# Moving columns read from the two halves of the operand in turn, on one Trainium2 core

## The chip, the core and the metric

The kernel runs on one core of a Trainium2 chip. The time is device microseconds (us) of one execution. A core has TensorE (PE; its weight loads are listed apart, as PEld), VectorE (DVE), ScalarE (ACT), GpSimd (POOL) and SyncE (SP, here the queue that issues the loads). A TensorE product holds 128 columns of one operand in the array (the stationary one, put there by a weight load) and streams the other through it column by column (the moving one); each moving column gives one column of sums in PSUM, at the place that the output pattern gives it. All operands lie in SBUF, 128 partitions by some number of 4-byte elements.

## The reference, cut to what matters

Two attention layers and a third block with a gated feed-forward net, on 256 tokens of width 2048. Nearly all arithmetic is in the products of activations with weights:

```python
# first block, twice (l = 0, 1)
h = x @ w_in                                  # (256, 2048) @ (2048, 6672)
# y_a, y_b, y_m: band attention, gated linear attention, memory attention
...
mkv = mem @ w_mem_kv                          # (256, 2048) @ (2048, 1024)
y = jnp.concatenate([y_a * jax.nn.silu(a_z), y_b * jax.nn.silu(b_z), y_m * jax.nn.silu(m_z)], axis=-1)
x = layer_norm(DEEPNORM_ALPHA * x + y @ w_out, ln_g, ln_b)
# second block
h = rms_norm(x, norm_mix_pre)
proj = h @ w_in_2                             # (256, 2048) @ (2048, 11272)
# y_a: hgrn2 recurrence, y_b: forgetting attention
...
merged = jax.nn.sigmoid(g_a) * (y_a @ w_up_a) + jax.nn.sigmoid(g_b) * (y_b @ w_up_b)
x = x + rms_norm(merged @ w_o, norm_mix_post)
gate, up = jnp.split(rms_norm(x, norm_ffn_pre) @ w_ffn_in, 2, axis=-1)      # width 2 * 5632
x = x + rms_norm((jax.nn.silu(gate) * up) @ w_ffn_down, norm_ffn_post)
```

## The kernel before

All inputs are float32. Each operand of a large product is split into a high part (rounded to the type fp32r, which TensorE takes in one pass) and the low rest, `hi + lo`, and a product is three: hi times hi, lo times hi, hi times lo. The activations lie in a `Split` tensor (`xx`, `yy`, `mem`), in which each tile of 128 features has 256 columns of high part (one a token) and then 256 of low part. Weights come by a load of 512 KB into one of five `raw` buffers; ACT makes the high part (`make_hi`, L441, `wh`) and DVE the low one (`make_lo`, L613, `wl`), each into one of four buffers.

There are two forms of large product. In **form f** (`unit_f`) the weights are stationary and the activations move, and a row of the sums is an output feature: `hi_row` moves `act.both(k)`, the 512 columns of high and low part, and `lo_row` moves `act.hi_of(k)`, 256 columns, onto the second half of the bank. The true sum is then the first half of the bank plus the second. In **form t** (`unit_t`, `last_rows`) the activations are stationary and 512 columns of `wh` or `wl` move, and a row of the sums is a token. `narrow` is form f for 16 or 8 output columns. All go through `add` (L283), so that L283 in the profile is every large product. A product is one matmul instruction of 128x512 or 128x256. Small products (attention scores, L368; transposes, L379; values, L387; the levels of the linear attention, `level`, L407) take plain float32 and go other ways; in the profile each of their instructions has two records.

The sums of form f are read by `join`: ACT copies the second halves of two banks into the destination (L460) and DVE adds the first halves (L638, or L640 where a factor is wanted). Those of form t are read by `evacuate` (L465 ACT, L648 DVE), `scale_value` (L574 ACT), `add_layer` (L780 DVE), `weigh_post` (L865 DVE) and `first_product` (L884 DVE); those of `narrow` by `narrow_sum`. Column c of a bank is column c of what moved. Products fill the bank pairs 0-1 and 2-3 by turns, so that a pair is read while the other is filled.

One place in the kernel of before already moves columns that do not lie side by side. `level(a, s, ...)` moves, in the third block, the second half of every group of `2*s` columns, for s = 64, 32, 16, 8, 4, 2, 1 and then (no s) all columns: 64 columns in runs of s. `merge_level` (L750) then reads PSUM in the same runs with a COPY_PREDICATED on DVE, and `differences` (L724, L725) reads and writes SBUF in such runs.

The order of the instructions on each engine is the order in which the program text issues them. Nothing is planned from costs.

Of the kernel before, what the change touches and what calls it, by code (L numbers as in the profile page):

```python
# [6 lines left out]
D, S, P = 2048, 256, 128  # L7
# [4 lines left out]
ALPHA = float(np.float32(4.0 ** 0.25))  # L12
# [49 lines left out]
class Split:  # L62
# [14 lines left out]
        return self.part(k, n, 1)  # L77

    def both(self, k):
        k += self.first  # L80
        return self.tensor[:, 2 * S * k:2 * S * (k + 1)]

    def hi_of(self, k, c=0, n=S):
        k += self.first
# [5 lines left out]

def tiled(x):
    return x.rearrange("p (k s) -> p k s", s=S)

def halves(x, s):
# [65 lines left out]
def build(nc, A, out):  # L161
    f32, f32r, i32 = mybir.dt.float32, mybir.dt.float32r, mybir.dt.int32
    ALU, ACT, AX = mybir.AluOpType, mybir.ActivationFunctionType, mybir.AxisListType
    ctx = ExitStack()
    with ctx:
# [59 lines left out]
        pairs = [ctx.enter_context(nc.psum_tensor(f"banks{n}", [P, 1024], f32)) for n in range(4)]  # L225
        banks = [pairs[n // 2][:, 512 * (n % 2):512 * (n % 2) + 512] for n in range(8)]
# [33 lines left out]
        def over2(row):  # L260
            return row.rearrange("p (o s) -> p o s", o=1).to_broadcast([P, 2, S])
# [6 lines left out]

        def of_bank_pair(pr):

            return pairs[pr[0] // 2][:, :].rearrange("p (t o s) -> p t o s", t=2, o=2)

        class Tensor(Part):

# [10 lines left out]
            def unit_f(self, h, l, act, pr, u, nu, made_hi, made_lo, free, hi_read, lo_read):  # L285

                def hi_row(*waits):
                    self.wait_ge(made_hi, *waits)
                    for kk in range(4):  # L290
                        k = 4 * u + kk
                        for t in range(2):
                            c = kk * S + t * P
                            i = self.add(banks[pr[t]], h[:, c:c + P], act.both(k), k == 0, k == 4 * nu - 1 and u % 2 == 1)
                    i.then_inc(hi_read.sem, 1)

                def lo_row(*waits):
                    self.wait_ge(made_lo, *waits)
                    for kk in range(4):
                        k = 4 * u + kk  # L300
                        for t in range(2):
                            c = kk * S + t * P
                            i = self.add(banks[pr[t]][:, S:2 * S], l[:, c:c + P], act.hi_of(k), False,
                                         k == 4 * nu - 1 and u % 2 == 0)
                    i.then_inc(lo_read.sem, 1)

                if u % 2 == 0:
                    hi_row(*free)
                    lo_row()
                else:  # L310
                    lo_row(*free)
                    hi_row()

            def unit_t(self, h, l, tiles, made_hi, made_lo, free, hi_read, lo_read):

                self.wait_ge(made_hi, *free)
                for b, act, t, k, place, start, _ in tiles:
                    m = h[:, place * 512:place * 512 + 512]
                    self.add(banks[b], act.hi_of(k, t * P, P), m, start, False)
                    i = self.add(banks[b], act.lo_of(k, t * P, P), m, False, False)  # L320
                i.then_inc(hi_read.sem, 1)
                self.wait_ge(made_lo)
                for b, act, t, k, place, _, stop in tiles:
                    i = self.add(banks[b], act.hi_of(k, t * P, P), l[:, place * 512:place * 512 + 512], False, stop)
                i.then_inc(lo_read.sem, 1)

            def last_rows(self, tiles, free, done):

                self.wait_ge(*free)
                for b, act, t, k, place, h, l, stop in tiles:  # L330
                    c = slice(place * 512, place * 512 + 512)
                    self.add(banks[b], act.hi_of(k, t * P, P), h[:, c], False, False)
                    self.add(banks[b], act.lo_of(k, t * P, P), h[:, c], False, False)
                    i = self.add(banks[b], act.hi_of(k, t * P, P), l[:, c], False, stop)
                i.then_inc(done.sem, 1)

            def narrow(self, bank, weights, act, free, done):
# [92 lines left out]
        class Scalar(Part):  # L430
# [26 lines left out]

            def join(self, pr, dst, scale, row, summed, free, copied, sums):
                self.wait_ge(summed, *free)
                self.e.activation(tiled(dst), of_bank_pair(pr)[:, :, 1, :], ACT.Copy,  # L460
                                  scale=1.0 if scale is None else scale).then_inc(copied.sem, 1)

            def evacuate(self, pr, dst, summed, first, second):
                self.wait_ge(summed)
                self.e.activation(dst[:, 0:512], banks[pr[0]], ACT.Copy).then_inc(first.sem, 1)  # L465

            def narrow_sum(self, b, n, dst, tmp, bias, row, summed, free, copied, sums):
                self.wait_ge(summed, *free)
                self.e.activation(dst, banks[b][0:n, S:2 * S], ACT.Copy).then_inc(copied[0].sem, 1)
                self.e.activation(tmp, banks[b][32:32 + n, 0:S], ACT.Copy).then_inc(copied[1].sem, 1)  # L470

            def exp_of_minus_abs(self, z, tmp, made, free, steps):
                self.wait_ge(*made, *free)
# [97 lines left out]

            def scale_value(self, o, b, factor, summed, free, done):
                self.wait_ge(summed, factor[1], *free)
                self.e.activation(o, banks[b], ACT.Identity, scale=factor[0]).then_inc(done.sem, 1)  # L574

            def forget_exps(self, u, tmp, made, first, second):
                self.wait_ge(made)
# [27 lines left out]
        class Vector(Part):  # L605
# [26 lines left out]
                self.e.tensor_scalar(lb[4], lb[3], -1.0, 1.0, ALU.mult, ALU.add).then_inc(made[6].sem, 1)  # L632

            def join(self, pr, dst, scale, row, summed, free, copied, sums):
                d, first = tiled(dst), of_bank_pair(pr)[:, :, 0, :]
                self.wait_ge(copied)
                if scale is None:
                    self.e.tensor_tensor(d, first, d, ALU.add).then_inc(sums[0].sem, 1)  # L638
                else:
                    self.e.scalar_tensor_tensor(out=d, in0=first, scalar=scale, in1=d, op0=ALU.mult,  # L640
                                                op1=ALU.add).then_inc(sums[0].sem, 1)
                if row is not None:
                    self.wait_ge(sums[0], row[1])
                    self.e.tensor_tensor(d, d, over2(row[0]), ALU.mult).then_inc(sums[1].sem, 1)

            def evacuate(self, pr, dst, summed, first, second):
                self.wait_ge(summed)
                self.e.tensor_copy(dst[:, 512:1024], banks[pr[1]]).then_inc(second.sem, 1)  # L648

            def narrow_sum(self, b, n, dst, tmp, bias, row, summed, free, copied, sums):  # L650
                self.wait_ge(copied[0])
                self.e.tensor_tensor(dst, banks[b][0:n, 0:S], dst, ALU.add).then_inc(sums[0].sem, 1)
                self.wait_ge(copied[1], sums[0])
                self.e.tensor_tensor(dst, dst, tmp, ALU.add).then_inc(sums[1].sem, 1)
                if bias is not None:
                    self.wait_ge(sums[1], row[1])
                    self.e.tensor_tensor(dst, dst, row[0][0:n, :], ALU.mult).then_inc(sums[2].sem, 1)
                    self.wait_ge(sums[2])
                    self.e.tensor_scalar(dst, dst, bias, None, ALU.add).then_inc(sums[3].sem, 1)
# [117 lines left out]

            def add_layer(self, z, bank, stats, summed, loaded, added, taken):
                self.wait_ge(summed, *loaded)
                self.e.scalar_tensor_tensor(out=z, in0=z, scalar=ALPHA, in1=banks[bank], op0=ALU.mult, op1=ALU.add).then_inc(added.sem, 1)  # L780
                self.wait_ge(added)
                self.e.bn_stats(stats, z).then_inc(taken.sem, 1)

# [78 lines left out]

            def weigh_post(self, o, b, w, made, done):
                self.wait_ge(*made)
                self.e.tensor_tensor(o, banks[b], w, ALU.mult).then_inc(done.sem, 1)  # L865

            def sum_squares(self, total, parts, made, done):
                self.wait_ge(*made)
# [6 lines left out]
            def gate_half(self, u, z, row, sigmoid, made, done):  # L875
                self.wait_ge(sigmoid)
                self.e.tensor_tensor(u, z, u, ALU.mult).then_inc(made.sem, 1)
                if row is not None:
                    self.wait_ge(made, row[1])
                    self.e.tensor_tensor(tiled(u), tiled(u), over2(row[0]), ALU.mult).then_inc(done.sem, 1)  # L880

            def first_product(self, o, b, factor, u, made, done):
                self.wait_ge(*made)
                self.e.scalar_tensor_tensor(out=o, in0=banks[b], scalar=factor[0], in1=u, op0=ALU.mult, op1=ALU.mult).then_inc(done.sem, 1)  # L884

        class Gpsimd(Part):

# [1621 lines left out]
```

## Time and profile before

| | us |
|---|---|
| median of 3 runs | 2407.21 (2406.29 to 2407.24) |
| profiled execution | 2406.68 |
| its span, first to last instruction | 2404.9 |
| PE busy in it | 2392.9 |
| DVE busy | 1541.9 |
| ACT busy | 1283.0 |

The profile page gives busy time of each engine, the span in 40 slices, and groups of instructions by line. A record of a matmul covers more than the time for which it holds the engine, since one begins before the last one's end: how long a product takes of TensorE's time is seen in a stretch of many, from start to start.

### The profile page before, as it was taken

To read this page: it belongs to the slowest core of one execution; us is meant where nothing else is said; L and a number is where in the kernel's file an instruction comes from. 1 tells how busy PE (TensorE), PEld (TensorE's weight loads), DVE (VectorE), ACT (ScalarE), POOL (GpSimd) and SP (SyncE) were. 2 spreads that over 40 slices of the span, in tenths; PEclk is the share of its full clock that TensorE was granted. 3 is DMA by queue.
4 is the path that set the end of the run, shared out by engine and by line. 5 is a ranking of instruction groups with operands and counts; after the bars stand their busy time and mean duration, and the time that the engine had idled before them with its cause. 6 is when DMAs were issued, how large, how long until landed. Compare 5 with 4: busy or idle time off the path is not lost.

```text
span 2404.9 us, 32960 instructions
## 1 busy us (share of the span) xinstructions
PE 2392.9 (99%) x13053; PEld 2067.0 (86%) x13053; DVE 1541.9 (64%) x1753; ACT 1283.0 (53%) x1741; POOL 12.3 (1%) x17
## 2 busy tenths in 40 slices
PE   9999999999999999999999999999999999999998
PEld 7888888888888888888888888888888888888887
DVE  6566567665665777686675567766666666665555
ACT  5444566444445654656654457555655555554444
POOL 0000000000000000000000000000000000000000
PEclk9999999999999999999999999999999999999999
DMA  8545447665445574554454545585555556557554
GB/s 305 198 151 165 166 164 266 214 223 186 157 142 178 189 285 144 197 187 153 167 175 152 174 157 184 188 284 186 183 193 193 184 184 202 183 194 251 195 192 141
DMA packets 130058, 458.84 MB, mean 191 GB/s; under 512 B 13776, under 2 KB 20464, under 8 KB 127984
## 3 DMA queue, kind: packets, MB, share of 16 engines
q1 hardware_dynamic: 128944, 450.39, 55.3%
q0 software_dynamic: 816, 6.29, 0.7%
q8 instruction: 102, 1.67, 0.3%
q14 instruction: 52, 0.43, 0.1%
q10 hardware_dynamic: 144, 0.07, 0.0%
HBM read 448.30 MB, written 8.39 MB: 190 GB/s over the span
## 4 chain that ended last, share of the span: by engine, by line
PE 97%; DVE 2%; ACT 1%; issue 0%; DMA 0%; SPq 0%; DVEq 0%; ACTq 0%
PE banks L283 91%; PE banks L407 2%; PE banks L387 1%; PE banks L368 1%; DVE wl L613 1%; PE banks L347 1%; PE banks L379 0%; ACT wh L441 0%; DMA raw<-in_kv_t 0%; DVE yy L617 0%; PE banks L418 0%; PE banks L419 0%; PE banks L417 0%; PE banks L395 0%; DVE b L775 0%
## 5 line engine op out<-in xcount | busy, mean ns | idle before, releaser
L613 DVE TENSOR_TENSOR wl<-raw,wh 128x1024 fp32r<-128x1024 f32 x776 | 938.2, 1221 | 410.5 <-ACT wh L441 405.0
L441 ACT ACTIVATE wh<-raw 128x1024 fp32r<-128x1024 f32 (+1 forms) x779 | 803.2, 1051 | 358.8 <-PE banks L283 209.6
L283 PE MATMUL banks<-xx,wh 128*128 128x512 f32 (+1 forms) x3760 | 906.6, 392 | 0.0
L283 PEld LDWEIGHTS banks<-xx,wh 128*128 128x128 f32 (+1 forms) x3760 | 686.0, 187 | 137.6 <-issue 0.7
L283 PEld LDWEIGHTS banks<-xx,wl 128*128 128x128 f32 x3712 | 479.9, 191 | 20.7 <-DVE wl L613 1.2
L283 PE MATMUL banks<-xx,wl 128*128 128x256 f32 x3712 | 495.0, 284 | 0.6 <-DVE wl L613 0.5
L283 PE MATMUL banks<-wh,xx 128*128 128x512 f32 x1504 | 376.5, 390 | 0.0
L283 PEld LDWEIGHTS banks<-wh,xx 128*128 128x128 f32 x1504 | 280.9, 188 | 57.6
L283 PE MATMUL banks<-wl,xx 128*128 128x512 f32 x752 | 204.0, 389 | 0.0
L283 PEld LDWEIGHTS banks<-wl,xx 128*128 128x128 f32 x752 | 141.2, 188 | 29.4
L283 PE MATMUL banks<-wh,yy 128*128 128x512 f32 x416 | 103.2, 389 | 0.0
L283 PEld LDWEIGHTS banks<-wh,yy 128*128 128x128 f32 x416 | 78.0, 188 | 16.2
L283 PE MATMUL banks<-yy,wh 128*128 128x512 f32 x256 | 61.2, 391 | 0.0
L283 PE MATMUL banks<-wl,yy 128*128 128x512 f32 x208 | 55.9, 389 | 0.0
L283 PEld LDWEIGHTS banks<-yy,wh 128*128 128x128 f32 x256 | 47.0, 188 | 9.1
L460 ACT ACTIVATE z<-banks 128x512 f32<-128x512 f32 x24 | 14.3, 598 | 74.4 <-PE banks L283 71.8
L460 ACT ACTIVATE hraw<-banks 128x512 f32<-128x512 f32 x20 | 12.0, 598 | 77.1 <-PE banks L283 77.1
L613 DVE TENSOR_TENSOR xl<-raw,xh 128x1024 fp32r<-128x1024 f32 x32 | 38.6, 1222 | 21.2 <-ACT xh L441 20.8
L441 ACT ACTIVATE xh<-raw 128x1024 fp32r<-128x1024 f32 x32 | 33.3, 1059 | 31.0 <-PE banks L283 17.2
L638 DVE TENSOR_TENSOR hraw<-banks,hraw 128x512 f32<-128x512 f32 x20 | 13.9, 693 | 54.6 <-ACT hraw L460 54.6
L283 PEld LDWEIGHTS banks<-wl,yy 128*128 128x128 f32 x208 | 39.1, 188 | 8.1
L638 DVE TENSOR_TENSOR z<-banks,z 128x512 f32<-128x512 f32 x24 | 16.6, 692 | 44.8 <-ACT z L460 44.8
(280 smaller groups left out, 1882.1 us busy)
## 6 DMA issues: line engine op xcount, KB each, us to landing
raw<-in_w_in_f SPq DMA_DIRECT2D x304, 512.0 KB, 3.4
raw<-in_w_ffn_f SPq DMA_DIRECT2D x160, 512.0 KB, 3.9
raw<-in_w_ffn_down SPq DMA_DIRECT2D x88, 512.0 KB, 4.3
raw<-in_w_in_t SPq DMA_DIRECT2D x80, 512.0 KB, 3.4
raw<-in_w_out_t SPq DMA_DIRECT2D x64, 512.0 KB, 4.8
raw<-in_w_o_t SPq DMA_DIRECT2D x32, 512.0 KB, 4.5
raw<-in_kv_t SPq DMA_DIRECT2D x16, 512.0 KB, 5.3
raw<-in_kv_f SPq DMA_DIRECT2D x16, 512.0 KB, 5.3
```

The source lines that it names most:

```text
L283: return self.e.matmul(bank, stationary, moving, start=start, stop=stop, skip_group_check=True)
L347: i = self.e.transpose(banks[bank][:, j * P:(j + 1) * P], tile, ident)
L368: i = self.e.matmul(o, a.q(h)[:, t * P:t * P + P], a.k(h)[:, 0:nk], start=True, stop=a.decay is None)
L387: i = self.e.matmul(banks[4][:, h * P:(h + 1) * P], a.v(kt, h), pt, start=(kt == 0), stop=(kt == nt - 1))
L407: j = self.e.matmul(part(banks[6 + i][:, n * P:(n + 1) * P]), lk[r, c:c + P], part(rq[r, c:c + P]), start=True, stop=True)
L441: self.e.activation(hi, source, ACT.Copy).then_inc(done.sem, 1)
L460: self.e.activation(tiled(dst), of_bank_pair(pr)[:, :, 1, :], ACT.Copy, scale=1.0 if scale is None else scale).then_inc(copied.sem, 1)
L613: self.e.tensor_tensor(lo, source, hi.bitcast(f32), ALU.subtract).then_inc(done.sem, 1)
L638: self.e.tensor_tensor(d, first, d, ALU.add).then_inc(sums[0].sem, 1)
```

## The change

Every large product takes its moving columns in another order. `in_turn` views n columns as two halves and takes column 0 of the first half, column 0 of the second, column 1 of the first, and so on. `act.both(k)` becomes the high part in turn and then the low part in turn (halves of 128 columns, so each column lies 512 bytes from the one before); `act.hi_of(k)` becomes `act.hi_in_turn(k)` in `lo_row`; in form t the 512 columns of weights are read in turn (halves of 256 columns, 1,024 bytes apart). The count of columns, the stationary operands, the PSUM addresses written and the sums are the same, but column 2b + a of a bank now holds what was column b of half a. So every reader of such a bank views it with `in_order`, reading each second element, and views what it writes `by_half`; in SBUF all stays where it was. `join` with a factor needs a pattern of more dimensions than the instruction has, and is written as two instructions of half the size (six places, L640). The order of instructions on all engines is otherwise the same.

```diff
     def both(self, k):
         k += self.first
-        return self.tensor[:, 2 * S * k:2 * S * (k + 1)]
+        return self.tensor[:, 2 * S * k:2 * S * (k + 1)].rearrange("p (o a b) -> p o b a", o=2, a=2)
+
+    def hi_in_turn(self, k):
+        return in_turn(self.hi_of(k))
...
+def in_turn(x):
+    return x.rearrange("p (a b) -> p b a", a=2)
+
+def in_order(x):
+    return x.rearrange("p (b a) -> p a b", a=2)
+
+def by_half(x):
+    return x.rearrange("p (a b) -> p a b", a=2)
+
+def tiled_by_half(x):
+    return x.rearrange("p (k a b) -> p k a b", a=2, b=P)
...
         def of_bank_pair(pr):
-            return pairs[pr[0] // 2][:, :].rearrange("p (t o s) -> p t o s", t=2, o=2)
+            return pairs[pr[0] // 2][:, :].rearrange("p (t o b a) -> p t o a b", t=2, o=2, a=2)
...
@@ unit_f @@
-                            i = self.add(banks[pr[t]][:, S:2 * S], l[:, c:c + P], act.hi_of(k), False,
+                            i = self.add(banks[pr[t]][:, S:2 * S], l[:, c:c + P], act.hi_in_turn(k), False,
...
@@ unit_t @@
-                    m = h[:, place * 512:place * 512 + 512]
+                    m = in_turn(h[:, place * 512:place * 512 + 512])
...
-                    i = self.add(banks[b], act.hi_of(k, t * P, P), l[:, place * 512:place * 512 + 512], False, stop)
+                    i = self.add(banks[b], act.hi_of(k, t * P, P), in_turn(l[:, place * 512:place * 512 + 512]), False, stop)
...
@@ join, ACT @@
-                self.e.activation(tiled(dst), of_bank_pair(pr)[:, :, 1, :], ACT.Copy,
+                self.e.activation(tiled_by_half(dst), of_bank_pair(pr)[:, :, 1, :, :], ACT.Copy,
...
@@ join, DVE @@
-                d, first = tiled(dst), of_bank_pair(pr)[:, :, 0, :]
+                d, first = tiled_by_half(dst), of_bank_pair(pr)[:, :, 0, :, :]
...
-                    self.e.scalar_tensor_tensor(out=d, in0=first, scalar=scale, in1=d, op0=ALU.mult,
-                                                op1=ALU.add).then_inc(sums[0].sem, 1)
+                    for k in range(2):
+                        i = self.e.scalar_tensor_tensor(out=d[:, k], in0=first[:, k], scalar=scale, in1=d[:, k], op0=ALU.mult,
+                                                        op1=ALU.add)
+                    i.then_inc(sums[0].sem, 1)
...
@@ add_layer; evacuate, scale_value, weigh_post, first_product and narrow_sum are changed alike @@
-                self.e.scalar_tensor_tensor(out=z, in0=z, scalar=ALPHA, in1=banks[bank], op0=ALU.mult, op1=ALU.add).then_inc(added.sem, 1)
+                self.e.scalar_tensor_tensor(out=by_half(z), in0=by_half(z), scalar=ALPHA, in1=in_order(banks[bank]), op0=ALU.mult,
+                                            op1=ALU.add).then_inc(added.sem, 1)
```

## Rows read from the trace of the kernel before

**Rows 1.** The page, busy time and share of the span by engine.

```profile
PE 2392.9 (99%) x13053; PEld 2067.0 (86%) x13053; DVE 1541.9 (64%) x1753; ACT 1283.0 (53%) x1741; POOL 12.3 (1%) x17
```

**Rows 2.** Busy time by stretch, L283 alone: start:end, length, busy (records), clock, DMA.

```profile
0.00:2405.00 2405.00, 2271.91 (x11792) 1932.09 (x11792) 1.00 0.56 191
```

**Rows 3.** Groups of instructions, shapes apart: the large products of 256 columns.

```profile
L283 PE MATMUL banks<-xx,wl 128*128 128x256 f32 x3712 | 495.0, 284 | 0.6 <-DVE wl L613 0.5
...
L283 PE MATMUL banks<-yy,wl 128*128 128x256 f32 x256 | 33.2, 283 | 0.0
...
L283 PE MATMUL banks<-mem,wl 128*128 128x256 f32 x128 | 17.6, 285 | 0.3
```

**Rows 4.** Timeline of PE: start us, length us, what, count.

```profile
258.27 2.08 PE L283 MATMUL banks<-xx,wl 128*128 128x256 f32 x16
...
2201.34 1.98 PE L283 MATMUL banks<-wh,xx 128*128 128x512 f32 x8
2203.15 1.07 PE L283 MATMUL banks<-wl,xx 128*128 128x512 f32 x4
```

**Rows 5.** One line's records, L283: duration ns min/median/max, first and last start.

```profile
L283 PE MATMUL banks<-xx,wl x3712: 277/283/468, 57.9 to 2155.9; 128*128 128x256 f32 x196
...
L283 PE MATMUL banks<-wl,xx x752: 388/389/400, 81.4 to 2396.9; 128*128 128x512 f32 x188
```

**Rows 6.** Small products on the timeline of PE: levels s = 64, 2, 1, and all columns.

```profile
1034.47 1.89 PE L407 MATMUL banks<-lqe 128*128 128x64 f32 x16
...
1112.56 1.90 PE L407 MATMUL banks<-lqe 128*128 128x64 f32 x16
1128.27 1.89 PE L407 MATMUL banks<-lqe 128*128 128x64 f32 x16
1135.66 1.95 PE L407 MATMUL banks<-q,k 128*128 128x128 f32 x16
```

**Rows 7.** One line's records: scores of 256 columns, and the first products of the program.

```profile
L368 PE MATMUL banks<-mk,q x8: 377/379/381, 628.1 to 629.6; 128*128 128x256 f32 x8
...
L279 PE MATMUL banks<-asleep x11: 390/628/792, 1.1 to 5.5; 128*128 128x512 f32 x11
```

**Rows 8.** Timeline of DVE, runs of 8, 4, 2 and 1 elements (L750), 4 and 1 (L724).

```profile
1083.10 0.76 DVE L750 COPY_PREDICATED lacc<-cst,banks 128x256 f32<-128x256 int32 x2 [2.98 <-PE banks L407]
1089.31 0.69 DVE L724 TENSOR_TENSOR le<-b 128x512 f32<-128x512 f32 x1
...
1100.16 0.76 DVE L750 COPY_PREDICATED lacc<-cst,banks 128x256 f32<-128x256 int32 x2
...
1115.49 1.33 DVE L750 COPY_PREDICATED lacc<-cst,banks 128x256 f32<-128x256 int32 x2
1118.37 0.70 DVE L724 TENSOR_TENSOR le<-b 128x512 f32<-128x512 f32 x1
...
1130.49 1.31 DVE L750 COPY_PREDICATED lacc<-cst,banks 128x256 f32<-128x256 int32 x2
```

**Rows 9.** Busy time by stretch: `join`'s copy L460 (ACT), its sum L638 (DVE).

```profile
0.00:2405.00 2405.00, 81.17 (x136) 1.00 0.56 191
...
0.00:2405.00 2405.00, 89.71 (x130) 1.00 0.56 191
```

**Rows 10.** What PE waited for: us in total, times, longest us.

```profile
PE banks L283 <- ACT wh L441: 1.2, 2, 0.9
...
PE banks L283 <- DVE wl L613: 0.5, 1, 0.5
```

**Rows 11.** Chain of work that ended last, in order of time: start us, us, what.

```profile
2394.85 2.51 PE banks L283 x11
...
2397.38 0.70 ACT junk L557 x2
...
2398.17 0.69 DVE o_buf L865
```

More of the change, by code:

```diff
@@ L331, in last_rows @@
                     c = slice(place * 512, place * 512 + 512)
-                    self.add(banks[b], act.hi_of(k, t * P, P), h[:, c], False, False)
-                    self.add(banks[b], act.lo_of(k, t * P, P), h[:, c], False, False)
-                    i = self.add(banks[b], act.hi_of(k, t * P, P), l[:, c], False, stop)
+                    self.add(banks[b], act.hi_of(k, t * P, P), in_turn(h[:, c]), False, False)
+                    self.add(banks[b], act.lo_of(k, t * P, P), in_turn(h[:, c]), False, False)
+                    i = self.add(banks[b], act.hi_of(k, t * P, P), in_turn(l[:, c]), False, stop)
                 i.then_inc(done.sem, 1)
@@ L464, in evacuate @@
                 self.wait_ge(summed)
-                self.e.activation(dst[:, 0:512], banks[pr[0]], ACT.Copy).then_inc(first.sem, 1)
+                self.e.activation(by_half(dst[:, 0:512]), in_order(banks[pr[0]]), ACT.Copy).then_inc(first.sem, 1)
             def narrow_sum(self, b, n, dst, tmp, bias, row, summed, free, copied, sums):
                 self.wait_ge(summed, *free)
-                self.e.activation(dst, banks[b][0:n, S:2 * S], ACT.Copy).then_inc(copied[0].sem, 1)
-                self.e.activation(tmp, banks[b][32:32 + n, 0:S], ACT.Copy).then_inc(copied[1].sem, 1)
+                self.e.activation(by_half(dst), in_order(banks[b][0:n, S:2 * S]), ACT.Copy).then_inc(copied[0].sem, 1)
+                self.e.activation(by_half(tmp), in_order(banks[b][32:32 + n, 0:S]), ACT.Copy).then_inc(copied[1].sem, 1)
             def exp_of_minus_abs(self, z, tmp, made, free, steps):
@@ L573, in scale_value @@
                 self.wait_ge(summed, factor[1], *free)
-                self.e.activation(o, banks[b], ACT.Identity, scale=factor[0]).then_inc(done.sem, 1)
+                self.e.activation(by_half(o), in_order(banks[b]), ACT.Identity, scale=factor[0]).then_inc(done.sem, 1)
             def forget_exps(self, u, tmp, made, first, second):
@@ L639, in join @@
                 else:
-                    self.e.scalar_tensor_tensor(out=d, in0=first, scalar=scale, in1=d, op0=ALU.mult,
-                                                op1=ALU.add).then_inc(sums[0].sem, 1)
+                    for k in range(2):
+                        i = self.e.scalar_tensor_tensor(out=d[:, k], in0=first[:, k], scalar=scale, in1=d[:, k], op0=ALU.mult,
+                                                        op1=ALU.add)
+                    i.then_inc(sums[0].sem, 1)
                 if row is not None:
                     self.wait_ge(sums[0], row[1])
+                    d = tiled(dst)
                     self.e.tensor_tensor(d, d, over2(row[0]), ALU.mult).then_inc(sums[1].sem, 1)
@@ L647, in evacuate @@
                 self.wait_ge(summed)
-                self.e.tensor_copy(dst[:, 512:1024], banks[pr[1]]).then_inc(second.sem, 1)
+                self.e.tensor_copy(by_half(dst[:, 512:1024]), in_order(banks[pr[1]])).then_inc(second.sem, 1)
             def narrow_sum(self, b, n, dst, tmp, bias, row, summed, free, copied, sums):
                 self.wait_ge(copied[0])
-                self.e.tensor_tensor(dst, banks[b][0:n, 0:S], dst, ALU.add).then_inc(sums[0].sem, 1)
+                self.e.tensor_tensor(by_half(dst), in_order(banks[b][0:n, 0:S]), by_half(dst), ALU.add).then_inc(sums[0].sem, 1)
                 self.wait_ge(copied[1], sums[0])
@@ L864, in weigh_post @@
                 self.wait_ge(*made)
-                self.e.tensor_tensor(o, banks[b], w, ALU.mult).then_inc(done.sem, 1)
+                self.e.tensor_tensor(by_half(o), in_order(banks[b]), by_half(w), ALU.mult).then_inc(done.sem, 1)
             def sum_squares(self, total, parts, made, done):
@@ L883, in first_product @@
                 self.wait_ge(*made)
-                self.e.scalar_tensor_tensor(out=o, in0=banks[b], scalar=factor[0], in1=u, op0=ALU.mult, op1=ALU.mult).then_inc(done.sem, 1)
+                self.e.scalar_tensor_tensor(out=by_half(o), in0=in_order(banks[b]), scalar=factor[0], in1=by_half(u), op0=ALU.mult,
+                                            op1=ALU.mult).then_inc(done.sem, 1)
         class Gpsimd(Part):
```

## The prediction

> **What bounds the kernel now.** I read the busy times first: PE is busy for 2392.9 us of a span of 2404.9, DVE for 64% of it and ACT for 53% [rows 1]. Then the waits: PE waits for ACT's and DVE's splitting of weights for 1.2 and 0.5 us in all [rows 10]. So the time is TensorE's own work, and nearly all of it is line 283, the large products, with 2271.9 us [rows 2]. What one costs is read from start to start. Sixteen products of 256 columns take 2.08 us, the last one's record being 0.283 us, so one takes (2.08 - 0.283) / 15 = 0.120 us. Eight of 512 columns take 1.98 us with a record of 0.389, so one takes (1.98 - 0.389) / 7 = 0.227 us [rows 4, 5]. The difference, 0.107 us for 256 columns, is 0.418 ns a column: the 2.4 GHz at which the clock stands in the whole run (1.00 in [rows 2]) is 0.417 ns a column. What is left, 0.120 - 0.107 = 0.013 us, is the same for both sizes: a fixed part of each product. In the count, 3,712 + 256 + 128 = 4,096 products have 256 columns [rows 3] and the other 11,792 - 4,096 = 7,696 have 512 [rows 2], which makes 4,096 x 256 + 7,696 x 512 = 4,989,000 moving columns. They come to 4.989 M x 0.417 ns = 2,079 us, and the fixed parts to 11,792 x 0.0133 = 157 us, 2,236 of the 2,272. **A column already goes at the array's own rate.** A new order of columns can't make it faster; it can only leave it, or slow it.
>
> **The moving reads.** All 4.989 M columns are now read from alternate places, 512 or 1,024 bytes apart. No row of before shows such a read. The bounds: from below, it costs nothing, since TensorE still asks for one element a column from each partition. From above, by the nearest rows: the levels of the linear attention move 64 columns in runs of s, and at s = 1 every second element. Their 16 records take 1.89 us at s = 64 and 1.89 at s = 1, and 1.95 with 128 columns side by side [rows 6]. That would look like "runs don't matter", but it isn't: since 64 and 128 columns take the same, something else sets the pace there, the weight load. What the row gives is a cap. A record takes (1.89 - 0.275) / 15 = 0.108 us, up to 0.112 by the row of 128 columns. A record of 256 columns in plain float32 takes (629.6 - 628.1) / 7 = 0.214 us [rows 7], twice the 0.107 of 256 columns in one pass, so a record is two passes, and the record at s = 1 reads 128 columns, in at most 0.112 us: 0.875 ns each. Elements that don't lie side by side could thus cost up to 2.1 times as much as now with nothing in this trace to show for it. The value between: 0.417 ns is the shortest time at which anything here takes an element (DVE takes 512 in 0.69 us, 1.35 ns each [rows 8]), and whatever the read path gives in pairs or lines of neighbours is needed most there. The natural loss is that a fetch which served two columns serves one, hence two cycles for a column, 0.833 ns. The other row at about that price is the first products of the program, 0.44 us from start to start for 512 columns, 0.86 ns each [rows 7]. I take 0.833: 4.989 M x (0.833 - 0.417) = **+2,079 us**. The cap gives 4.989 M x (0.875 - 0.417) = +2,285 us. The fixed 157 us stay.
>
> A sentence of the skill speaks for a loss. The Trainium skill, "Advanced Engine Details and Errata", section Memory Cachelines, says that SBUF has lines of 16 bytes, that at least two accesses should hit one line to hide the memory's latency, and that a different line for each access is penalised; "in turn" makes each access another line than the one before. It gives no price. At s = 1 above, steps of 8 bytes leave two hits in a line, so the trace neither agrees nor disagrees. Another speaks against it, and is the first rival.
>
> **The readers.** A bank is read at every second element. DVE's COPY_PREDICATED reads PSUM so in the levels: two of 256 elements take 0.76 us in runs of 8 and of 4, and 1.33 and 1.31 in runs of 2 and 1 [rows 8], so 0.57 us more for 512 elements. The other row, a TENSOR_TENSOR within SBUF, takes 0.69 us in runs of 4 and 0.70 in runs of 1 [rows 8]: nothing. So a read of 512 elements costs 0 to 0.57 us more. There are 130 + 6 sums of `join` (L638, L640), 8 copies, 16 + 16 + 2 others on DVE, 178, and on ACT 136 + 8 + 10 = 154 (L638 and L460 in [rows 9], the others by the order of the instructions): 0 to 101 us on DVE and 0 to 88 us on ACT. I take the middle, but it hardly counts. The cover is that a bank pair is filled while the other is read: form f fills a pair with 32 products of 512 columns and 32 of 256, 32 x 0.347 = 11.1 us, and one `join` is 0.60 + 0.69 = 1.3 us (81.17 / 136 and 89.71 / 130 [rows 9]), 2.4 at most. DVE would go from 64% to 68%. On the path are the last read of the kernel (L865, 0.69 us [rows 11]) and some ten places where a norm follows a product: 0 to 11 x 0.57 = 6 us, taken as 1. The six split instructions add six fixed parts on DVE, below 1 us together, and are covered too. If TensorE becomes twice as slow, everything on DVE, ACT and the loads has twice the time, and PE's present 12 us of idleness (2404.9 - 2392.9) may shrink: -6 us.
>
> **Sum.** Against the profiled execution's 2406.7 us, 0.5 below the median: 2406.7 + 2,079 + 1 - 6 = **4,481 us**, with 4,460 to 4,700 as its own range (the cap gives 4,687).
>
> **The rivals.** (1) *The hop is free*; it ends on the other side. TensorE's read stream keeps both places open, or its buffer fetches ahead, and a column stays at 0.417 ns. What remains is the readers: 2407.2 + 0 to 6, about 2,408 us. It decides if a read of 128 partitions by one element is no slower than by two neighbours. For it: L724 shows no loss in runs of 1 on DVE [rows 8], and only two streams alternate. Against it: L750 does lose [rows 8], and TensorE reads 3.2 times as fast as DVE. Beside it stands a rule: the Trainium skill, "Vector Engine (DVE) Microarchitecture Reference", section 5.2, tells that a one-source operation whose read stream alternated between two regions 16 KiB apart at every element went at the full read rate, though hops in other patterns cost some two thirds more. If TensorE's port behaves like that, this rival holds; no row here shows it. (2) *The fixed part goes.* If the 0.013 us of each product come from where its moving columns are read (a clash with the weight load that runs beside it), another order could save up to 157 us: 2,250 us. Against it: they are the same for 256 and 512 columns, and for activations and weights as the moving side (1.07 us for four of 512: (1.07 - 0.389) / 3 = 0.227 again [rows 4]), so they look like a change of weights, not like a clash of addresses. (3) *A hop costs TensorE what short runs cost L750*, 0.57 us / 512 = 1.1 ns an element: + 4.989 M x 1.1 = 5,550 us, about 7,960 us. For it: it is the only row in which short runs cost anything. Against it: the cap at s = 1 rules it out for steps of 8 bytes, though not for 512. (4) A loss of a part only, such as the first columns of each product: 2,450 to 4,400 us.
>
> **How the numbers follow.** Half rate 0.46; free 0.27; the fixed part shrinks 0.12; far worse than half rate 0.10; a part 0.05. The forecast is the likeliest, 4,481 us. The range has to leave out no more than 2 in 10: from 2,250 (rival 2's end, with rivals 1 and 4 in it) to 4,700, which leaves out rival 3 and what a wider miss of the price would be. It is wide because two answers lie 2,000 us apart with little between. A measurement of this kernel can tell about 0.2%, 5 us, from no change. Faster by more: 0.12 of rival 2 and 0.01 of rival 1; within: 0.20 of rival 1; slower: the rest of rival 1 (0.06, the readers on the path) and 0.61 of the others.
>
> **What would show it.** Half rate: eight products of 512 columns in a row take (1.98 - 0.39) x 440 / 227, some 3.1 us from first to last start instead of 1.6, sixteen of 256 columns 15 x 0.227 = 3.4 instead of 1.8; the weight loads' share falls from 86% to about 46%, DVE's to about 35%. Free: the same rows unchanged. The readers: L460 and L638 at 597 and 690 ns or up to 0.57 us more. The fixed part: 256 columns below 0.120 us by as much as 512 below 0.227. The prediction is wrong at its root if the price of a column doesn't follow from neighbours in SBUF, and in size if the fetch is wider than two elements.

## The result

The changed kernel takes 2289.84 us (2288.61 to 2291.24, four runs) where the kernel before takes 2407.22 (2406.29 to 2407.89): 0.9513 of it, with a 95% interval of 0.9496 to 0.9529. It is 117 us faster; the forecast was 2,074 us slower. The nearest of the prediction's times is that of rival 2, a smaller part beside the columns in each product.

The page of the profile after, busy time by engine (answers to [rows 1]), and the stretch of the whole run for the large products alone, which are line 305 now (answers to [rows 2]):

```profile
PE 2272.6 (99%) x13053; PEld 2044.5 (89%) x13053; DVE 1543.5 (67%) x1759; ACT 1278.3 (56%) x1741; POOL 12.3 (1%) x17
```

```profile
0.00:2290.00 2290.00, 2151.59 (x11792) 1910.91 (x11792) 1.00 0.61 200
```

The same number of products at the same granted clock (1.00) takes 2151.6 us instead of 2271.9. The timeline of PE of the kernel after (answers to [rows 4]) and two lines of its records (answers to [rows 5]) show where:

```profile
246.78 1.95 PE L305 MATMUL banks<-xx,wl 128*128 128x256 f32 x16
248.56 1.89 PE L305 MATMUL banks<-xx,wh 128*128 128x512 f32 x8
...
252.01 1.03 PE L305 MATMUL banks<-wl,xx 128*128 128x512 f32 x4
```

```profile
L305 PE MATMUL banks<-xx,wh x3760: 379/379/634, 51.0 to 2053.4; 128*128 128x512 f32 x195, 128*48 128x512 f32 x3
...
L305 PE MATMUL banks<-xx,wl x3712: 271/275/460, 56.1 to 2051.7; 128*128 128x256 f32 x196
```

A product of 512 columns takes (1.89 - 0.379) / 7 = 0.216 us from start to start, where it took 0.227; one of 256 columns takes (1.95 - 0.275) / 15 = 0.112, where it took 0.120. The sum closes: 7,696 x 0.011 + 4,096 x 0.008 = 85 + 33 = 118 us, and the times differ by 117. In the profiled executions the large products' busy time falls by 2271.9 - 2151.6 = 120.3 us, and PE's idle time grows from 2404.9 - 2392.9 = 12.0 us to 2289.2 - 2272.6 = 16.6.

The readers of the sums, which now take each second element of PSUM, cost nothing (the answers to [rows 9], in the form of one line's records; ACT's copy and DVE's sum in `join`):

```profile
L482 ACT ACTIVATE z<-banks x24: 592/597/601, 1340.0 to 2032.8; 128x512 f32<-128x512 f32 x24
```

```profile
L660 DVE TENSOR_TENSOR z<-banks,z x24: 682/692/692, 1340.6 to 2033.5; 128x512 f32<-128x512 f32 x24
```

They were at 597 and 690 ns on average before. PE still waits for ACT and DVE for a few microseconds only (2.0 and 2.8 us for the weights; 1.2 and 0.5 in [rows 10]).

### The profile page after: what moved, and what is told of

It is laid out like the page before. It is cut to its first block, busy times and chain, and to the rows that moved or that the text cites. A ratio compares the mean times of both kernels' runs of the same rounds, so it can differ in the third digit from the quotient of the medians.

```text
span 2289.2 us, 32966 instructions
## 1 busy us (share of the span) xinstructions
PE 2272.6 (99%) x13053; PEld 2044.5 (89%) x13053; DVE 1543.5 (67%) x1759; ACT 1278.3 (56%) x1741; POOL 12.3 (1%) x17
## 4 chain that ended last, share of the span: by engine, by line
PE 95%; DVE 2%; DMA 2%; ACT 1%; issue 0%; SPq 0%; DVEq 0%; ACTq 0%
PE banks L305 89%; PE banks L429 2%; PE banks L409 1%; PE banks L390 1%; DVE wl L635 1%; PE banks L369 1%; PE banks L401 0%; ACT wh L463 0%; DMA raw<-in_kv_f 0%; DMA w_bc<-in_norm_mix_post 0%; DMA raw<-in_memT 0%; DVE yy L639 0%; DMA raw<-in_xT 0%; DMA raw<-in_kv_t 0%; PE banks L441 0%
## 5 line engine op out<-in xcount | busy, mean ns | idle before, releaser
L305 PE MATMUL banks<-xx,wh 128*128 128x512 f32 (+1 forms) x3760 | 860.8, 380 | 0.0
L305 PEld LDWEIGHTS banks<-xx,wl 128*128 128x128 f32 x3712 | 456.2, 192 | 17.6 <-DVE wl L635 3.5
L305 PE MATMUL banks<-xx,wl 128*128 128x256 f32 x3712 | 466.5, 276 | 2.3 <-DVE wl L635 2.2
L305 PE MATMUL banks<-wh,xx 128*128 128x512 f32 x1504 | 359.9, 380 | 0.0
L305 PE MATMUL banks<-wl,xx 128*128 128x512 f32 x752 | 195.9, 379 | 0.0
L660 DVE TENSOR_TENSOR z<-banks,z 128x512 f32<-128x512 f32 x24 | 16.6, 691 | 37.9 <-ACT z L482 37.9
```

The lines of the kernel that those rows point to most:

```text
L305: return self.e.matmul(bank, stationary, moving, start=start, stop=stop, skip_group_check=True)
```

## The experiments

Two questions: which property of the moving order makes a product 11 ns quicker, and why the halves in turn, whose every element lies 512 or 1,024 bytes from the last, don't cost double. Three kernels that leave the computation out and run trains of products on an otherwise idle core ask this; four others are the whole kernel with a part of the change or another order.

### Trains of products, one order each

The edit is a kernel of its own. Each line issues 32 products, each with its own stationary tile and moving tile out of eight and seven, and each line has its own number in the profile:

```python
for i in range(N): e.matmul(B(i), W(i), M(i), **k)                 # plain 512
for i in range(N): e.matmul(B(i), W(i), turn(M(i)), **k)           # two halves in turn
for i in range(N): e.matmul(B(i), W(i), runs(M(i), 2), **k)        # halves in turn, by pairs of neighbours
...
```

> This kernel leaves the whole computation out: it runs trains of 32 products (64 in the first), each train on a line of its own, on an otherwise idle chip, and copies x to the output. Start to start per product is read. Known from the two kernels: plain 512 columns 227 ns, in turn 216; plain 256 120, in turn 112. Theory A, a clash of the moving read with the weight load that runs beside it: another order of the stationary read (every fourth column) moves the 227 as well, the same operands each time give less than 227, and 48 stationary columns give less than 128 do. Theory B, neighbours in the moving stream are what costs (each product pays for its first fetch of neighbours): pairs, runs of 4 and of 8 from two halves in turn stay at 227 or lie between, in turn and even-then-odd are at 216. Theory C, it is the pattern's number of dimensions and not the addresses: two far runs of 256 already give 216, and step 2 in one dimension stays at 227. Theory D, it is the other engines' traffic in the whole kernel: here plain and in turn are equal. In bfloat16 A and D expect a difference too; B and C say nothing.

The timeline of PE: start us, length us, line, count. From the start of one line to that of the next, divided by 32, is the time of a product. Lines 66 to 70 are the halves in turn by 1, 2, 4, 8 and 16 neighbours; 72 two far runs of 256; 73 each second column; 74 all even columns, then all odd; 75 the four quarters in turn; 88 the order 0, 4, 1, 5, 2, 6, 3, 7 within each group of 8; 89 plain, one element on. All are fp32r.

```profile
34.56 7.07 PE L66 MATMUL banks<-xr,wr 128*128 128x512 f32 x32
41.46 11.04 PE L67 MATMUL banks<-xr,wr 128*128 128x512 f32 x32
52.33 8.18 PE L68 MATMUL banks<-xr,wr 128*128 128x512 f32 x32
60.35 7.95 PE L69 MATMUL banks<-xr,wr 128*128 128x512 f32 x32
68.13 7.84 PE L70 MATMUL banks<-xr,wr 128*128 128x512 f32 x32
...
83.09 7.42 PE L72 MATMUL banks<-xr,wr 128*128 128x512 f32 x32
90.34 14.66 PE L73 MATMUL banks<-xr,wr 128*128 128x512 f32 x32
104.83 14.69 PE L74 MATMUL banks<-xr,wr 128*128 128x512 f32 x32
...
215.69 7.07 PE L88 MATMUL banks<-xr,wr 128*128 128x512 f32 x32
222.60 7.70 PE L89 MATMUL banks<-xr,wr 128*128 128x512 f32 x32
```

| moving order, fp32r, 512 columns | ns a product |
|---|---|
| plain | 227 to 228 |
| two halves in turn | 216 |
| halves in turn, by pairs / by 4 / by 8 / by 16 / by 64 | 340 / 251 / 243 / 240 / 228 |
| two far runs of 256 | 227 |
| each second column; all even, then all odd | 453; 453 |
| quarters in turn; 64 parts in turn | 274; 431 |
| 0, 4, 1, 5, 2, 6, 3, 7 within each 8 | 216 |
| plain, the same operands each time; same stationary; same moving | 227; 227; 227 |

Theory D (traffic of the other engines) falls: alone on the core the two orders differ by the same 11 ns. Theory C (the number of dimensions) falls by line 72, which has two dimensions and 227 ns. Theory A, the clash with the weight load, is weakened: the same operands each time take 227 ns like any others, and 48 stationary columns take 236 ns plain, more and not less. (Its other part told nothing: with a stationary tile read at steps a product takes 233 to 238 ns, and 234 even with 256 moving columns, so something else than the moving read sets the pace there.) Theory B expected pairs between 216 and 227, and they take 340, and even-then-odd at 216, which takes 453: it falls as it was put. So neighbours in the stream don't hurt as such, and a hop doesn't either; what they have to do with each other was open.

### Two streams

Column by column, halves in turn looks like the worst order for a memory that gives neighbours together. Looked at as two streams, the columns with even numbers and those with odd ones, it is the best: each walks through neighbours. Plain gives each stream every second element. This kernel tells the two views apart; its trains read, among others:

```python
# halves in turn, step 2 in each: even columns 0, 2, 4, ...; odd columns 512, 514, ...
xr[:, c:c + 1024].rearrange("p (a b c) -> p b a c", a=2, c=2)[:, :, :, 0]
# in turn within each 4: 0, 2, 1, 3
M(i).rearrange("p (g a b) -> p g b a", a=2, b=2)
```

> Like m1_patterns this kernel leaves the whole computation out and runs trains of 32 products. Seen there: plain 227 ns for 512 columns, in turn 216, pairs of neighbours from the two halves 340, runs of 4 250, step 2 453. Theory S (two streams): TensorE fetches the even columns and the odd columns of the moving operand as two streams, each of which is quick if its own elements are neighbours and slow if each lies in another piece of memory. It expects: halves in turn with step 2 in each like plain (227), with step 4 in each like step 2 (some 450), in turn within 4 elements (0, 2, 1, 3: each stream goes in pairs) like plain or worse, within 16, 32 and 128 like the halves (216), eighths in turn slower than 272. Theory O (one stream, where alternation as such is free): halves in turn with step 2 like step 2 alone (453). For the fixed 11 ns: if they are a clash with the weight load, they shrink with fewer stationary columns (16 columns: below 218) and don't grow with the moving columns (264 plain 11 over 264 in turn); if they are the stream's own, they grow with the moving columns (384: 8, 264: 6). Start one to sixteen elements on: by a clash of addresses between moving and stationary reads, something between 216 and 240 that depends on the start; in turn 216 at each start.

The timeline of PE again; 75, 76, 77 and 79 are plain with 480, 448, 384 and 264 columns, 80 and 82 in turn with 384 and 264, 83 plain, one element on; 90 is in turn within each 4 columns, 91 within each 16, 92 within each 32, 95 eighths in turn, 96 halves in turn with step 2 in each, 97 the same with step 4, 98 step 4 alone:

```profile
92.48 7.10 PE L75 MATMUL banks<-xr,wr 128*128 128x480 f32 x32
99.42 6.65 PE L76 MATMUL banks<-xr,wr 128*128 128x448 f32 x32
105.91 5.73 PE L77 MATMUL banks<-xr,wr 128*128 128x384 f32 x32
...
116.17 4.05 PE L79 MATMUL banks<-xr,wr 128*128 128x264 f32 x32
120.05 5.36 PE L80 MATMUL banks<-xr,wr 128*128 128x384 f32 x32
...
129.60 3.76 PE L82 MATMUL banks<-xr,wr 128*128 128x264 f32 x32
133.20 7.71 PE L83 MATMUL banks<-xr,wr 128*128 128x512 f32 x32
...
184.26 7.46 PE L90 MATMUL banks<-xr,wr 128*128 128x512 f32 x32
191.55 7.07 PE L91 MATMUL banks<-xr,wr 128*128 128x512 f32 x32
198.46 7.07 PE L92 MATMUL banks<-xr,wr 128*128 128x512 f32 x32
...
220.87 15.83 PE L95 MATMUL banks<-xr,wr 128*128 128x512 f32 x32
236.52 7.45 PE L96 MATMUL banks<-xr,wr 128*128 128x512 f32 x32
243.81 14.66 PE L97 MATMUL banks<-xr,wr 128*128 128x512 f32 x32
258.29 14.94 PE L98 MATMUL banks<-xr,wr 128*128 128x512 f32 x32
```

Line 96 is the one that decides: (243.81 - 236.52) / 32 = 228 ns, as much as plain, where step 2 as one stream costs 453. With step 4 in each half, one element in 16 bytes for each stream, it is (258.29 - 243.81) / 32 = 453, and step 4 as one stream takes 461. Within each 4, where each stream goes in pairs, it is 228, and within each 16, 32 and 128 it is 216. Eighths in turn take 489, slower than the 272 that theory S set as the least. Theory S holds in all of these, and theory O falls. A memory that keeps two places open at once, but has one stream, isn't enough either: plain would then be as quick as in turn.

The 11 ns don't shrink with fewer stationary columns (16, 32, 64 and 96 take 231, 232, 230 and 230 ns plain, and 32 and 96 in turn 216): no clash that grows with the weight load. With fewer moving columns, plain against in turn is 174.1 to 162.5 at 384, 146.6 to 135.9 at 320 and 121.3 to 112.5 at 264: 11.6, 10.7 and 8.8 ns. From 384 to 264 the loss shrinks by 3 ns, as the expectation of a cost of the read's own had it (8 and 6), but it is 3 ns larger at each. The plain times of 264 to 480 columns lie on a line: (216.9 - 121.3) / 216 = 0.443 ns a column, and those in turn have (162.5 - 112.5) / 120 = 0.417. So a plain column costs more than one in turn, and only the step from 480 to 512 breaks this, 216.9 to 227, 10 ns where the line gives 14. Starts 1, 2, 4, 8 and 16 elements on take 236, 233, 232, 233 and 229 ns plain, but 217 and 216 in turn for 1 and 2: whatever disturbs the plain read there leaves the read in turn alone.

### The two forms apart

Only form f with `narrow`, and then only form t, each with its own readers:

```diff
 # e_form_f, against the changed kernel: form t as before
-                    m = in_turn(h[:, place * 512:place * 512 + 512])
+                    m = h[:, place * 512:place * 512 + 512]
 # e_form_t, against the kernel before: form t changed
-                    m = h[:, place * 512:place * 512 + 512]
+                    m = in_turn(h[:, place * 512:place * 512 + 512])
```

> Only form f, narrow included, and its readers have the change; form t is as before. Per product 11 ns for 512 columns and 8 for 256, off a TensorE that never waits: (3,760 + 256 + 128) x 11 + 4,096 x 8 = 46 + 33 = 78 us saved, 2,329 us, 0.967 of before. If the gain came from somewhere else than each product's own time (say, from how the readers or the loads fall), it doesn't follow this count.

> Only form t and its readers have the change. By the same count (7,696 - 4,144) x 11 = 39 us saved, 2,368 us, 0.984 of before. With e_form_f it should make the whole 117 us.

Form f alone: 2326.78 us, 0.9669 (0.9655 to 0.9684), 80 us saved for 78 expected. Form t alone: 2368.99 us, 0.9844 (0.9828 to 0.9861), 38 saved for 39 expected. Together 118. In the timeline of PE of the kernel with form f alone both prices stand side by side, 1.89 us for eight with the activations moving and 1.98 with the weights moving:

```profile
250.51 1.89 PE L305 MATMUL banks<-xx,wh 128*128 128x512 f32 x8
252.25 1.98 PE L305 MATMUL banks<-wh,xx 128*128 128x512 f32 x8
```

So the gain is made in each product, in either form.

### A hop of 16 bytes, and one of 8

The whole kernel, with each group of 8 columns as 0, 4, 1, 5, 2, 6, 3, 7, and then each group of 4 as 0, 2, 1, 3. The readers are those of before, so both kernels leave out putting the sums back in the order of the columns.

```diff
+def in_eights(x):
+    return x.rearrange("p (g a b) -> p g b a", a=2, b=4)      # in e_fours: a=2, b=2
...
-                    m = h[:, place * 512:place * 512 + 512]
+                    m = in_eights(h[:, place * 512:place * 512 + 512])
```

> All large products take each group of 8 columns as 0, 4, 1, 5, 2, 6, 3, 7, so hops are of 16 bytes, not 512 or 1,024; the readers are those of before, so the sums stay in that order: what is left out is putting the columns in order. If only alternation counts and the readers cost nothing, 2,290 us as in the changed kernel; if the readers cost their 0.57 us for 512 elements anywhere on the path, below it by up to 6 us; if the distance of the hop counts, near 2,407.

> All large products take each group of 4 columns as 0, 2, 1, 3, a hop of 8 bytes; the readers are those of before, so what is left out is putting the columns in order. By the picture of two streams each stream still finds only two of its elements in 16 bytes, so nothing is gained: 2,407 us, within 0.3%. If alternation or the number of dimensions of the pattern were what counts, 2,290 us as with groups of 8.

Groups of 8: 2288.21 us, 0.9509 (0.9495 to 0.9524), the changed kernel's time (0.9513), and without its readers of every second element: they cost nothing that can be measured. Groups of 4: 2406.27 us, 1.000 (0.9991 to 1.001). Both kernels hop at every column and both patterns have three dimensions. What differs is that with 8 each stream finds four of its elements in 16 bytes, with 4 only two, as plain. The timelines of PE of the two, groups of 8 and then groups of 4:

```profile
246.77 1.95 PE L287 MATMUL banks<-xx,wl 128*128 128x256 f32 x16
```

```profile
258.20 2.08 PE L287 MATMUL banks<-xx,wl 128*128 128x256 f32 x16
260.12 2.00 PE L287 MATMUL banks<-xx,wh 128*128 128x512 f32 x8
```

### What a piece of 16 bytes costs, and what the 11 ns are

```python
for i in range(N): j = e.matmul(B(i), W(i), M(i), **k); j = e.matmul(B(i), W(i), turn(M(i)), **k)   # by turns
...
# halves in turn, step 3 in each
xr[:, 0:1536].rearrange("p (a b c) -> p b a c", a=2, c=3)[:, :, :, 0]
```

> Like the two kernels of trains before, this leaves the whole computation out. Working picture from them: the even and the odd moving columns are two streams; each takes memory in pieces of 16 bytes, one piece in 0.833 ns, so that a product of 512 needs 128 pieces in turn (107 ns), 256 plain (213 ns, exactly as long as the array's own 213), 512 with steps of 16 bytes in each stream (427, measured 453). Predicted by it: halves in turn with step 3 in each, 384 pieces: 320 to 347 ns; step 3 and step 6 like step 4, some 453. For the fixed 11 ns of a plain product there are two theories. F1, the read keeps pace with the array but has nothing to spare, so what is lost where one product follows another is never made up: then a plain product after one in turn is helped by what that one's quick read has saved, and plain and in turn by turns take 216 + 216 to 222 a pair. F2, each product with a plain read pays it by itself: the pair takes 227 + 216 = 443, two plain and one in turn 670, three and one 897. In bfloat16 a pair of elements is 4 bytes: by the picture bf16 in turn by pairs is as quick as plain (216); if the hop as such hurts bf16 it stays at 484.

The timeline of PE: 66 plain, 67 in turn, 68 the two by turns, 69 two plain and one in turn, 70 three plain and one in turn; 71 plain of 512 and plain of 64 columns by turns, 72 in turn of 512 and plain of 64, 73 plain of 512 and plain of 256; 75 plain of 512 and in turn of 256, 76 both in turn; 77 halves in turn with step 3 in each, 78 step 3 alone, 79 step 6 in each half; in bfloat16 84 plain, 85 in turn, 86 and 87 in turn by pairs and by fours, 88 in turn within each 16, 89 in turn within each 4:

```profile
25.98 7.42 PE L66 MATMUL banks<-xr,wr 128*128 128x512 f32 x32
33.23 7.07 PE L67 MATMUL banks<-xr,wr 128*128 128x512 f32 x32
40.14 14.46 PE L68 MATMUL banks<-xr,wr 128*128 128x512 f32 x64
54.44 21.71 PE L69 MATMUL banks<-xr,wr 128*128 128x512 f32 x96
75.98 28.96 PE L70 MATMUL banks<-xr,wr 128*128 128x512 f32 x128
104.78 11.04 PE L71 MATMUL banks<-xr,wr 128*128 128x512 f32 x64
115.66 10.64 PE L72 MATMUL banks<-xr,wr 128*128 128x512 f32 x64
126.13 11.34 PE L73 MATMUL banks<-xr,wr 128*128 128x512 f32 x64
...
148.07 11.04 PE L75 MATMUL banks<-xr,wr 128*128 128x512 f32 x64
158.96 10.64 PE L76 MATMUL banks<-xr,wr 128*128 128x512 f32 x64
169.43 11.05 PE L77 MATMUL banks<-xr,wr 128*128 128x512 f32 x32
180.31 14.57 PE L78 MATMUL banks<-xr,wr 128*128 128x512 f32 x32
194.70 14.58 PE L79 MATMUL banks<-xr,wr 128*128 128x512 f32 x32
...
229.43 7.08 PE L84 MATMUL banks<-xb,wb 128*128 128x512 bf16 x32
236.35 15.66 PE L85 MATMUL banks<-xb,wb 128*128 128x512 bf16 x32
251.85 8.84 PE L86 MATMUL banks<-xb,wb 128*128 128x512 bf16 x32
260.52 7.42 PE L87 MATMUL banks<-xb,wb 128*128 128x512 bf16 x32
267.78 15.70 PE L88 MATMUL banks<-xb,wb 128*128 128x512 bf16 x32
283.31 7.07 PE L89 MATMUL banks<-xb,wb 128*128 128x512 bf16 x32
```

Step 3 in each half takes (180.31 - 169.43) / 32 = 340 ns, inside the 320 to 347 expected, and step 3 alone 450. So in fp32r, where each stream walks forward through one place, the price follows the number of 16-byte pieces that the two streams touch: 128 pieces 216 ns, 256 pieces 227, 384 pieces 340, 512 pieces 453. The last three stand as 2 : 3 : 4 to each other, 0.886 ns a piece. At that price the first would be 113; what it takes instead is the time of 512 columns at 0.417 ns, 213, and 2.5. The orders in which one stream goes back and forth among places lie off this count: in turn by 4, 8 and 16 neighbours takes 251, 243 and 240 where 256 pieces would give 227, and 64 parts in turn takes 431 and eighths 489 where 512 would give 453.

Theory F1, that the lost time could be made up by the neighbour's quick read, falls: plain and in turn by turns take (54.44 - 40.14) / 32 = 447 ns a pair, not 432 to 438, two plain with one in turn (75.98 - 54.44) / 32 = 673, and three with one (104.78 - 75.98) / 32 = 900; F2 expected 443, 670 and 897. Each plain product pays for itself, as F2 says, and each round takes some 4 ns more, which isn't explained.

In bfloat16 plain takes 216 ns already, and the halves in turn take 484, more than double. Pairs, which by the picture should have been as quick as plain, take 271, fours 227, in turn within each 16 takes 485, and of the orders in turn only 0, 2, 1, 3 is free, 216. The picture of two streams with pieces of 16 bytes holds for 4-byte elements and not for these. What holds for them was not found.

## Why the prediction was wrong

**What bounds the kernel**: right in the main. The count of products (11,792, of which 4,096 with 256 columns) and the claim that TensorE's own work sets the time are what the result is made of. The split of a product isn't borne out. The prediction took 0.418 ns a column and a fixed 13 ns from two sizes, 256 and 512, and concluded that a new order of columns can't make a column faster; between 264 and 480 a plain column costs 0.443 ns and one in turn 0.417. The 157 us that were to stay are where the 117 us came from.

**The moving reads**: wrong, and this is the step that failed. The sentence "the natural loss is that a fetch which served two columns serves one, hence two cycles for a column" took neighbours in the moving order for what a fetch serves. The trains fit a fetch that serves a stream of every second column. On that reading halves in turn don't halve what a fetch of 16 bytes gives, they double it, from two elements to four. The price I gave, double, does exist: 453 ns for 512 columns, for each second column, where a stream gets one element from 16 bytes. It went to the wrong pattern. The term of the sum was +2,079 us and should have been some -118, with nothing for it in the term of the fixed parts. The other row that the prediction set beside its price, 0.44 us for each of the first products [rows 7], says nothing of the order: in the first train, m1_patterns, 64 plain products at the start of TensorE's work begin at much the same pace and end at the usual one, with their columns side by side and the clock column at 1.00 throughout (busy time by stretch, PE; a product that reaches over an edge counts on both sides):

```profile
17.50:19.50 2.00, 2.00 (x5) 1.00 0.00 0
...
29.50:31.50 2.00, 2.00 (x11) 1.00 0.00 0
```

**The row read as a cap** ([rows 6], s = 1, at most 0.875 ns a column) held nearly: step 2 costs 453 / 512 = 0.885 ns a column in fp32r, 1% above it. The row is of plain float32, which no train ran, so that the weight load hid such a price there is likely and not shown. The row was about a step of 2, which costs; the change makes a hop between halves, which doesn't.

**The rule weighed.** The Trainium skill, "Advanced Engine Details and Errata", section Memory Cachelines, wants at least two hits on a line of 16 bytes and penalises a new line for each access. In fp32r the trains agree with its figure if the hits are counted in each of the two streams: 4 and 2 hits give 216 and 227 ns, 1.33 and 1 give 340 and 453. Counted along the order of columns, as I did, it gives the wrong sign. The section also says of PSUM that any pattern that isn't contiguous slows matmuls. No run here shows that, since the products write PSUM side by side in every kernel; ACT's and DVE's reads of every second element of PSUM cost nothing, 597 and 692 ns.

**The readers**: within their bounds, at the lower end. 597 and 692 ns after, 597 and 690 before. The row that gave the upper end, COPY_PREDICATED in short runs [rows 8], doesn't carry over to ACTIVATE and TENSOR_TENSOR. The split sums of `join` take 0.41 us for each half where one instruction took 0.69, off TensorE's path.

**Rival 1** (the hop is free) was right on the hop and missed the gain. **Rival 2** had the time nearest to it, 2,250 us at its end, but its reason, a clash with the weight load, isn't borne out: fewer stationary columns don't help. The argument against it, that the part is the same for 256 and 512 columns and for either operand and so looks like a change of weights, was the second error: two sizes don't show that a cost is fixed, and the sizes between them have another slope. **Rival 3** is far off for this pattern; a column cost at most 0.96 ns in any order tried (489 ns for eighths in turn).

**The chances**: the measured time lies in the range, near its lower end, because rival 2's end was taken in. That is luck of the width, not a sign of the mechanism. The direction was forecast wrongly, with 0.13 on faster.

## What to carry to other kernels

On a TensorE that never waits, the order in which a product reads its moving columns is worth a train of 32 products on an idle core before it is argued about: here 4-byte operands gained 11 ns of 227 from reading two places in turn, and 2-byte operands lost a factor of 2.2 from the same edit. For fp32r, let the even and the odd columns each walk through neighbours; the two places need only be 16 bytes apart, so the reordering can stay within groups of 8 columns. The reader of the sums can take each second element of PSUM at no cost, with ACTIVATE and TENSOR_TENSOR at least; a reader that puts groups of 8 back in order was not run.
